# A trunk kernel in fp32: modulation tiles multiplied one at a time, scratch cleared behind the masks, turned keys one job later

## The reference, cut to what matters

```python
mod_x = jnp.split((jax.nn.silu(c) @ w_mod + b_mod)[:, None, :], 6, axis=-1)
mod_c = jnp.split((jax.nn.silu(c_ctx) @ w_mod + b_mod)[None, None, :], 6, axis=-1)
hc = modulate(rmsnorm(ctx, norm1_g), mod_c[0], mod_c[1])
fc, qc, kc, vc, zc, gc, bc = mixer_features(hc, w_in, conv_w, a_log, dt_bias, conv_seq)
oc, s_fwd, s_bwd = bidir_delta(qc, kc, vc, gc, bc, zero_state, zero_state)
hx = modulate(rmsnorm(x, norm1_g), mod_x[0], mod_x[1])
fx, qx, kx, vx, zx, gx, bx = mixer_features(hx, w_in, conv_w, a_log, dt_bias, conv_grid)
ox, _, _ = bidir_delta(qx, kx, vx, gx, bx, s_fwd, s_bwd)
x = x + mod_x[2] * mixer_output(fx, ox, zx, onorm_g, w_out)
x = x + mod_x[5] * moe_ffn(modulate(rmsnorm(x, norm2_g), mod_x[3], mod_x[4]), ...)
```

## Time and profile before

| | us |
|---|---|
| median of 3 runs | 1940.42 |
| lowest, highest | 1935.62, 1940.86 |
| the profiled execution, its own time | 1938.43 |
| its span, first to last instruction | 1936.6 |
| PE busy | 1811.5 (94%) |
| PE weight load busy | 1409.7 (73%) |
| DVE, ACT, POOL busy | 508.0, 422.8, 74.8 |
| mean granted PE clock | 0.967 |
| bytes moved by DMA | 383.32 MB, mean 198 GB/s |

### The profile page before, as it was taken

How to read it: one execution, slowest core, us unless ns; L and a number is a source line. 1 busy time by engine, 2 the same in 40 slices (tenths; PEclk the granted TensorE clock), 3 DMA queues, 4 the chain that set the end, 5 groups by cost and what they waited for, 6 DMA issues and landing times.

```text
span 1936.6 us, 24878 instructions
## 1 busy us (share of the span) xinstructions
PE 1811.5 (94%) x10310; PEld 1409.7 (73%) x10310; DVE 508.0 (26%) x1143; ACT 422.8 (22%) x907; POOL 74.8 (4%) x72
## 2 busy tenths in 40 slices
PE   4987878799999999999999999999999999899997
PEld 2674757566666665678678888888887688788886
DVE  3749432400100100022430312121135312212113
ACT  1532211211110110121442221111224522211112
POOL 0251000100000000010000100000000000000000
PEclk9988889799999999999999999999999999899999
DMA  9111256299999999983322323444433133234420
GB/s 393 41 44 44 82 224 261 111 398 422 422 422 422 422 421 422 422 332 134 123 85 109 130 106 134 152 152 152 151 137 131 44 130 109 87 131 152 152 87 22
DMA packets 53645, 383.32 MB, mean 198 GB/s; under 512 B 6208, under 2 KB 6336, under 8 KB 7360
## 3 DMA queue, kind: packets, MB, share of 16 engines
q1 hardware_dynamic: 52272, 376.97, 49.4%
q10 hardware_dynamic: 1296, 5.24, 0.7%
HBM read 381.14 MB, written 1.05 MB: 197 GB/s over the span
## 4 chain that ended last, share of the span: by engine, by line
PE 86%; DVE 6%; DMA 3%; ACT 2%; POOL 1%; issue 1%; SPq 0%; DVEq 0%; ACTq 0%
PE ps L576 83%; DMA ring<-in_stream 3%; PE ps L574 2%; PE ps L631 1%; DVE ring L1929 1%; POOL ring L460 1%; DVE arena L1935 1%; DVE arena L1929 1%; ACT arena L1693 0%; DVE small L2405 0%; DVE arena L1932 0%; DVE ring L2068 0%; ACT L1445 0%; DVE arena L2303 0%; DVE arena L1943 0%
## 5 line engine op out<-in xcount | busy, mean ns | idle before, releaser
L576 PE MATMUL ps<-arena,ring 128*128 128x256 f32 (+2 forms) x3680 | 833.7, 388 | 12.6 <-DVE arena L1932 5.8
L576 PEld LDWEIGHTS ps<-arena,ring 128*128 128x128 f32 x3680 | 697.1, 193 | 139.8 <-issue 46.7
L576 PE MATMUL ps<-ring,arena 128*64 128x256 f32 (+4 forms) x3168 | 485.0, 419 | 0.0
L576 PEld LDWEIGHTS ps<-ring,arena 128*64 128x64 f32 (+1 forms) x3168 | 294.1, 148 | 174.6 <-issue 84.5
L576 PE MATMUL ps<-arena 128*128 128x128 f32 (+5 forms) x1256 | 203.5, 322 | 6.9 <-DVE rounds_i L2259 2.2
L576 PEld LDWEIGHTS ps<-arena 128*128 128x128 f32 (+3 forms) x1256 | 167.4, 189 | 39.3 <-issue 24.5
L1935 DVE SCALAR_TENSOR_TENSOR arena<-ps,par,arena 128x255 f32<-128x255 f32 (+1 forms) x178 | 74.3, 479 | 336.7 <-ACT arena L1905 335.5
L576 PE MATMUL ps<-ring 128*128 128x256 f32 (+2 forms) x896 | 116.8, 302 | 12.6 <-DVE ring L2078 8.9
L576 PEld LDWEIGHTS ps<-ring 128*128 128x128 f32 (+2 forms) x896 | 99.4, 164 | 26.4 <-DVE ring L2078 9.7
L1905 ACT ACTIVATE arena<-ps,par 128x256 f32<-128x256 f32 x88 | 42.4, 563 | 313.5 <-PE ps L576 313.5
L576 PE MATMUL ps<-arena,cst 128*128 128x256 f32 (+1 forms) x308 | 88.6, 433 | 11.7 <-ACT arena L1721 5.4
(11 more groups left out here) (175 smaller groups left out, 796.3 us busy)
## 6 DMA issues: line engine op xcount, KB each, us to landing
ring<-in_stream SPq DMA_DIRECT2D x358, 1024.0 KB, 10.5
arena<-in_xc ACTq DMA_DIRECT2D x1, 1024.0 KB, 5.1
xT<-in_xc ACTq DMA_DIRECT2D x1, 1024.0 KB, 8.8
arena<-in_mem ACTq DMA_DIRECT2D x1, 1024.0 KB, 4.8
out_y<-xT ACTq DMA_DIRECT2D x2, 512.0 KB, 2.7
ring<-in_dft ACTq DMA_DIRECT2D x1, 512.0 KB, 8.0
arena<-in_sguw ACTq DMA_DIRECT2D x2, 256.0 KB, 2.8
par<-in_par SPq DMA_DIRECT2D x1, 511.5 KB, 24.6
```

The costliest lines, as they stand in the source:

```text
L576: i = nc.tensor.matmul(out, lhsT, rhs, start=start, stop=stop, skip_group_check=skip)
```

## The change

It consists of four parts.

1. Modulation goes tile by tile. `mod_cols(i)` waits for one tile and issues 8 products; chunk c goes to column group c % 4, so that four chunks run side by side and each group adds up two. Four part sums of both vectors now lie in the bank. `mod_turn(i)` joins them: instead of two transposes it issues two products of the copied row (128 x 128 stationary) with `selv`, a 128 x 2 constant that picks and adds the rows, and writes 2 columns behind the first 256 of the bank. `mod_unit(i)` is the columns of tile i and the turn of tile i - 1. Eight units stand at the start, with the sums of squares behind the third; sixteen are spread between the steps of the delta rule. The bias is added once behind the eight, and once behind the sixteen. Each row copy is now one per tile (24 instead of 6).
2. The clearing of `bB` and `bF`, with its wait for tile 11, stands behind the eight masks in POOL's program.
3. PE turns the keys back one job later: one half of the first `job_b` tile goes ahead of it; the keys' product moves back likewise.
4. Tiles 12 on go to slot (n - 12 + 2) % 4, each waiting for its own slot's tile; the expert tiles 8 to 11 wait for one of the tiles 34 to 37 each.

```diff
         def pre_slot(n):
-            return n if n < SLOTS else (n - SLOTS) % BASE
+            return n if n < SLOTS else (n - SLOTS + 2) % BASE
...
             for n in range(SLOTS, S_PRE):
-                sp.wait_ge(free, n - SLOTS + 1 if n < SLOTS + BASE else n - BASE + 1)
+                sp.wait_ge(free, pre_slot(n) + 1 if n < SLOTS + BASE else n - BASE + 1)
...
-                    sp.wait_ge(free, S_PRE)
+                    sp.wait_ge(free, S_PRE - SLOTS + j + 1)
...
-            pool.wait_ge(free, SLOTS)
-            nc.gpsimd.memset(bB, 0.0)
-            nc.gpsimd.memset(bF, 0.0).then_inc(fill_ok, 1)
-
...
             for c in range(4, 8):
                 mask(c)
+            pool.wait_ge(free, SLOTS)
+            nc.gpsimd.memset(bB, 0.0)
+            nc.gpsimd.memset(bF, 0.0).then_inc(fill_ok, 1)
...
+            def mod_cols(i):
+
+                s = arrive()
+                if i not in (0, 1, S_MOD_A, S_MOD_A + 1):
+                    pe.wait_ge(modrow_ok, i - 1)
                 for c in range(KC):
-                    for q in range(4):
-                        i = nc.tensor.matmul(bank(MOD_BANK[groups[0]], T)[32 * q:32 * q + 32, :], silu_c[:, c, :],
-                                             wB(pre_slot(pos[0] + q), c, 0, T), start=c == 0, stop=c == KC - 1,
-                                             tile_position=(0, 32 * q))
...
+                    q = 32 * (c % 4)
+                    mi = nc.tensor.matmul(mod_at(i)[q:q + 32, 0:T], silu_c[:, c, :], wB(s, c, 0, T),
+                                          start=c < 4, stop=c >= 4, tile_position=(0, q))
+                mi.then_inc(mod_ps, 1)
+                release()
+
+            def mod_turn(i):
+
+                pe.wait_ge(modrow_ok, i + 1)
+                row_ = (modrow_a if i < S_MOD_A else modrow_b)[i % 2]
                 for k in range(2):
-                    mm(bank(MOD_BANK[g], T)[:, k * P:k * P + P], modrow[g][:, k * P:k * P + P], ident, tr=True,
-                       inc=modt_ps if k else None)
+                    at = T + 4 * (i // 2 if i < S_MOD_A else (i - S_MOD_A) // 2) + 2 * k
+                    mm(mod_at(i)[:, at:at + 2], row_[:, k * P:k * P + P], C("selv"), inc=modt_ps if k else None)
...
-            mod_columns()
-            for g in range(2):
-                mod_turn(g)
+            for i in range(S_MOD_A):
+                mod_unit(i)
+                if i == 2:
+                    pe.wait_ge(sq_ok, 1)
+                    for c in range(KC):
+                        mm(bank(4, 2 * T), ones, sqA[:, c, :], c == 0, c == KC - 1, ss_ps if c == KC - 1 else None)
+            mod_turn(S_MOD_A - 1)
...
             solve(0)
-            pe.wait_ge(vt_ok, 3)
             for t in range(TT):
                 turns(t, lambda hd: qT[:, hd, tok(t)], tr_k)
+            mod_unit(10)
             state_add(0)
-            mod_turn(2)
-            pe.wait_ge(vt_ok, 4)
-            mod_columns()
+            mod_unit(11)
+            mod_unit(12)
...
             state_keys(3)
             out_state(3)
-            mod_turn(5)
+            mod_unit(20)
+            mod_unit(21)
             solve(3)
+            mod_unit(22)
+            mod_unit(23)
             out_values(3)
+            mod_turn(23)
...
             residual(3)
-            mod_add(5)
-            dve.wait_ge(mods_ok, 6)
+            mod_add(S_MOD_A, S_MOD_B, (7, 2))
+            dve.wait_ge(mods_ok, 4)
```

More of the change, by code:

```diff
@@ L736, in _ @@
             job_b(s, hA, T + P, 0, T)
-            release()
-            s = arrive()
-            for t in range(TT):
-                job_b(s, hA, T + t * P, 0, T)
             release()
@@ L1634, in _ @@
                 A_(vtok[:, t], bank((7, 0, 1, 2)[t], H1, P), ACT.Copy).then_inc(vt_ok, 1)
-            mod_rows(2)
-            mod_rows(3)
+            for i in range(8, 13):
+                mod_rows(i)
             for t in range(TT):
@@ L1639, in _, with queries, new_values @@
                 A_(qT[:, :, t * P:t * P + P], bank(t, H1, P), ACT.Copy).then_inc(norm_ok, 1)
[L1640 to L1644 removed]
+            for i in range(13, 17):
+                mod_rows(i)
+            def queries(ks):
+                for k in ks:
+                    act.wait_ge(tr_k, 10 + k + 1)
+                    A_(qE[:, k], bank(k % 2, H1, P), ACT.Copy).then_inc(qe_ok, 1)
+            def new_values(s):
                 for d in range(2):
@@ L1650, in _ @@
                     A_(bV[:, d], bank(4 + 2 * d, H1, P), ACT.Copy).then_inc(vc_ok, 1)
-                if s == 2:
-                    mod_rows(5)
+            queries((0, 1))
+            mod_rows(17)
+            queries((2, 3))
+            new_values(2)
+            for i in range(18, 22):
+                mod_rows(i)
+            new_values(3)
+            for i in range(22, 24):
+                mod_rows(i)
             for i, t in enumerate((1, 0)):
```

113 lines of the change are left out of this document (53 added, 60 removed).

## The result

Both kernels ran side by side. The changed kernel takes 1925.27 us (median of 6 runs, 1921.68 to 1929.4), the kernel before 1936.39 (6 runs, 1928.41 to 1940.86): a ratio of 0.9947, 95% interval 0.9929 to 0.9965. That is 11.1 us less by the medians and 10.3 by the ratio, more than the 0.3% that a measurement tells. The profiled executions have spans of 1936.6 and 1926.2 us at mean clocks of 0.967 and 0.971.

The account below looks back on a forecast made before the run. PE's chain of waits (83% of the span) was taken to bound most stages, with waits on other engines in the first 307 us. -4.8 + 1.5 - 10.5 = -13.8 on 1938.43 gives 1924.6, plus 2.0 is 1926.6 us; range 1914 to 1938.

Parts of the forecast that it names:

- Start: Up to the first in-projection job: three units before the sums of squares, earlier job, less lower clock; -4.8 us (-2 to -7).
- the sums run from about 20.2 to 27.4: PE's sums of squares at the start, behind the new units: 4.1 us earlier than before.
- I take half back: -1.0: First in-projection job: 2.2 us of its 9.17 were lower clock; with less PE idle ahead, half is regained.
- Masks and keys: Up to the inverse and its copies: earlier masks hold DVE's convolutions, keys scaled 14.2 us later; +1.5 us (-13 to +8).
- beside the moved clears 2: DVE's query convolutions: only 2 steps done beside POOL's moved clears, at one step per POOL instruction.
- DVE decides again: 196.5 instead of 195.0: At the copies behind the inverse: PE waits for DVE, 1.5 us later than before.
- the masks' gain comes through: Rival (16%): masks hold DVE less; half the hold gone gives -6 there, total 1919, all gone 1912.
- Delta rule: Groups, DMA waits and transposes gone (37.8 us), 16 units added (25.1), 1.3 for waits, end +0.9; -10.5 us.
- Units were not dear: Rival (16% with late tiles): column-group passages or row copies cost more; at 2.2 us a unit +10, so 1937.
- tiles not late: Rival (within the 16% of dear units): tiles come late one by one, waits stay, worth 14.9 us; 1941.
- rival (c): Rival (8%): the clock falls in the delta rule over its 57 us of PE work; all of it would give 1984.
- last output product near 288 less 3.3: Sign for the end of the delta rule: when its last output product comes, on the old time scale.

Follow-up runs that it names:

- e4: Changed kernel plus extra products with unread results on PE at the start and 14 ahead of the inverse's second level; 1920.82 us, ratio 0.9921 to the kernel before.
- e10: Changed kernel with POOL's masks waiting until DVE has scaled the keys; 1916.43 us, ratio 0.9891 to the kernel before.
- e1: Changed kernel with clears back ahead of the masks and keys turned back where they were, leaving tile-by-tile modulation and its slots; 1919.75 us, ratio 0.9909 to before.
- e3: Changed kernel with DVE scaling the turned keys between the second and third query convolutions; 1913.31 us, ratio 0.9874 to the kernel before.
- e8: Kernel before with 20 extra products ahead of its first modulation group and 10 behind the last turn; 1930.24 us, ratio 0.9981 to the kernel before.

## Why the prediction was right or wrong

**Start, -4.8 predicted, +1.8 measured: wrong.** The order was read right: the sums at 20.70 (20.2), the second unit waiting for its row copy, units of 1.54 (1.57, though its own terms add up to 1.56). The step that failed is "the sums run from about 20.2 to 27.4". It took their 7.13 us from a place where a long group stood ahead of them; behind three short units they ran at the lower clock up to 25.50, 9.49 in all. So "first job at 38.1" became 40.57. The other failed step is "I take half back: -1.0": the job took 9.79 us, 0.6 more and not 1.0 less, and the clock fell again over the gates, which cost 2.5 us. The job's start 2.5 us late, 1.6 in the job and 2.5 in the gates are the 6.6 us by which this stretch missed. The prediction put the falls down to waits ("the falls I see followed 4 to 8 us without a product"); the one over the gates came with PE at work, in the kernel before too, and the sum had no term for it. e4 shows that the order is worth what was said when the clock is there.

**Masks and keys, +1.5 predicted, -0.3 measured: no gain, as said, by terms that were partly wrong.** POOL's masks, without their wait, held DVE one step per product, and e10 shows it by taking them away. PE's wait for the keys is 15.36 where 16.4 was walked. Wrong is "beside the moved clears 2": the clears held none of the SCALAR_TENSOR_TENSOR steps, so the keys came 12.0 us later behind the first step, not 14.2. That is 2.2 of walked loss that was not there, more than the 1.8 us between forecast and measurement. Against e1, where the constants lie as in the changed kernel, the part costs 1.5 at the inverse. And "DVE decides again: 196.5 instead of 195.0" has the right time (196.69), but what follows came later than it says: behind a PE wait of 7.77 us the level's products took 3.57 us instead of 2.79, at a granted clock of 0.50, and a gap of 0.75 followed, so the next job started 3.5 us late (201.26, before 197.72), not 1.5. The rival that the masks' gain comes through fell: none of it did. The part as a whole loses: without it (e1), or with the masks behind the keys (e10), the out-projection comes 4.8 and 5.2 us sooner, of which some 1.5 to 1.7 is the clock ahead of the delta rule, and the medians are 5.5 and 8.8 us lower.

**Delta rule, -10.5 predicted, -11.3 measured: right.** 16 units of 1.54 instead of 1.57 are 0.5 us less than the sum. The 1.3 us of waits were not there: PE was busy throughout. Together that is 1.8 saved, yet from the first column product to the last output product it takes 58.6 us, where the sum had 58.7 (70.1 - 12.7 + 1.3). Of what was lost 1.2 is the lower clock up to 237.1, over the first units, for which the sum had no term; the rest wasn't taken apart. The end cost 0.2 instead of 0.9 us, nearly all of the difference: from the last output product to the out-projection it was 5.73 before (307.19 - 301.46) and is 5.93 now (299.29 - 293.36). Units were not dear, tiles not late, and the clock rose in this stage (0.86 to 0.98): those three rivals fell there. What rival (c) feared happened, smaller, at the start. One of the signs fails by its own arithmetic: "last output product near 288 less 3.3" doesn't follow from the sum, which gives 301.46 - 11.4 - 3.3, or 286.8. It ended at 293.36, 6.6 later, about what the start missed.

**Behind it, 0 predicted, -2.5 measured.** At an expert copy of ACT's the gain is 8.93 us (397.42 to 388.49), and at the end 10.4. Part of the rest, about 1.4 us, is a dip of the clock in the execution of before, between 900 and 920 us; the changed kernel has 1.00 there. That belongs to the execution and not to the change. The row of before:

```profile
900.00:920.00 20.00, 20.00 (x87) 17.33 (x87) 8.88 (x18) 2.25 (x5) 0.00 (x0) 0.93 0.37 132
```

**The sum.** Against the -13.8 that was predicted: the start 6.6 worse, masks and keys 1.8 better, between the inverse and the delta rule 1.9 worse (the level's products and the gap behind them), the delta rule 0.8 better, behind it 2.5 better. That is 3.4 less gain by the traces (10.4), and 2.7 less by the medians (11.1). The median of before came out 4.0 lower, and 4.0 less 2.7 is the 1.3 us by which the forecast missed. The time was near by luck, because these two nearly cancel; of the gain it was a quarter too high by the medians, a third by the traces. The part that was read and sized right is the delta rule, which alone is as large as the whole gain.

## What to carry over

Work that frees one engine may only put two engines beside each other that hold one another: here POOL's masks ended 24 us earlier (143.6 to 119.1), DVE lost 12 us to them, and the gain came from reordering DVE (e3, 12.0 us by the medians, 9.4 behind the first step). Breaking a group that waits for four transfers into units that wait for one won back its full wait, because the units had other work between them; cost such a unit by its weight loads and column time, and check by doubling one instruction. And a duration of PE's may be carried to a new place only with the clock of that place.

## What was unexpected of the hardware

- A DVE TENSOR_SCALAR (SBUF to SBUF, 128x256, 0.35 us alone) took 3.72 to 4.08 us beside POOL's clears, through four of them in a row; SCALAR_TENSOR_TENSOR steps beside the same clears were hardly slowed, but took 1.22 us each beside POOL's TENSOR_TENSOR. Beside DVE these mostly took 1.15 to 1.22 us, alone 1.04 to 1.09.
- POOL's products with constants took 1090 instead of 1267 ns once the constants lay two columns further.
- Sixteen records of modulation columns take 1.94 us at 17.96 us and 1.07 at 30.12, while the granted clock in the windows is 1.00 for both. The trace has no clock record ahead of 25.50 us in the changed kernel and of 22.19 in the kernel before, and the column says 1.00 where it has none; the durations tell the lower level there. The sums took 8.56 to 10.15 us in the seven kernels that have the same program ahead of them; in each, 7.11 us and half of what lay at the lower level or ahead of the first full-clock record give the measured time within 0.03 us.
- A gap of 0.5 to 2.2 us, for which the trace names no releaser ("issue"), stands ahead of the last 32x32 products of the second level in the changed kernel and the experiments, e8 among them, and not in the profiled execution of before. Its cause is open.
